# A hybrid decoder trunk: chunks of the input projection computed in turn, small with large

## The reference

```python
h = _rmsnorm(x, attn_norm[l])
proj = jnp.einsum('bsd,de->bse', h, w_in[l])     # one projection, columns split:
# differential attention (6 heads), gated linear attention (4 heads),
# latent attention (6 heads, low-rank queries 512 and keys/values 256 + rotary key 64)
x = x + jnp.einsum('bse,ed->bsd', mixed, w_out[l])
h2 = _rmsnorm(x, ffn_norm[l])
ff = jax.nn.silu(h2 @ w_gate[l]) * (h2 @ w_up[l])
x = x + ff @ w_down[l]
```

## Time and profile before

| | us |
|---|---|
| median of 3 runs | 2172.93 (2172.77 to 2174.07) |
| profiled execution | 2175.64 |
| its span | 2172.3 |
| granted TensorE clock, mean | 0.999 |
| busy: TensorE | 2159.1 (99%) |
| busy: VectorE | 1715.9 (79%) |
| busy: ScalarE | 1083.0 (50%) |

### The profile page before, as it was taken

One profiled execution on the slowest core, in us unless ns is written; L12 is line 12 of the kernel. 1 busy time (PEld: TensorE's weight loads), 2 busy tenths in 40 slices (PEclk: granted clock), 3 DMA queues, 4 the chain that ended last, 5 costly groups with the idle time before them and its releaser, 6 DMA issues.

```text
span 2172.3 us, 27182 instructions
## 1 busy us (share of the span) xinstructions
PE 2159.1 (99%) x10826; PEld 1843.7 (85%) x10826; DVE 1715.9 (79%) x1939; ACT 1083.0 (50%) x1145; POOL 22.2 (1%) x24
## 2 busy tenths in 40 slices
PE   9999999999999999999999999999999999999998
PEld 8899988888888888888888999888888888888886
DVE  5676774788899888889755866747888898888887
ACT  6454543554554455445443645445554454445544
POOL 0000000000000000000000000000000000000000
PEclk9999999999999999999999999999999999999999
DMA  7543455556556665665554434555565655665664
GB/s 265 179 137 117 148 173 194 178 198 205 194 195 197 201 198 196 204 198 194 194 189 158 151 113 158 173 178 192 194 197 198 203 193 194 198 207 194 198 206 158
DMA packets 221679, 402.77 MB, mean 185 GB/s; under 512 B 13440, under 2 KB 53664, under 8 KB 221472
## 3 DMA queue, kind: packets, MB, share of 16 engines
q1 hardware_dynamic: 220880, 400.90, 56.2%
q10 hardware_dynamic: 720, 0.78, 0.1%
HBM read 399.54 MB, written 2.10 MB: 185 GB/s over the span
## 4 chain that ended last, share of the span: by engine, by line
PE 95%; DVE 2%; DMA 1%; issue 1%; ACT 1%; SPq 0%; DVEq 0%; POOLq 0%; POOL 0%; ACTq 0%
PE bank L1021 19%; PE bank L1023 19%; PE bank L1022 19%; PE bank L698 10%; PE bank L700 10%; PE bank L699 10%; PE bank L658 3%; PE bank L823 1%; DMA stage<-in_w_down 1%; PE bank L764 0%; PE bank L887 0%; DMA stage<-in_w_in 0%; DVE w_lo L1551 0%; PE bank L875 0%; PE bank L765 0%
## 5 line engine op out<-in xcount | busy, mean ns | idle before, releaser
L1551 DVE TENSOR_TENSOR w_lo<-stage,w_hi 128x2048 fp32r<-128x2048 f32 (+4 forms) x318 | 678.0, 2134 | 266.7 <-ACT w_hi L1185 266.4
L1185 ACT ACTIVATE w_hi<-stage 128x2048 fp32r<-128x2048 f32 (+4 forms) x318 | 567.4, 1786 | 384.4 <-DMA stage<-in_w_down 191.3
L698 PE MATMUL bank<-w_hi,xt_hi 128*128 128x512 f32 (+4 forms) x1048 | 375.9, 359 | 2.0 <-DVE w_lo L1551 2.0
L700 PE MATMUL bank<-w_hi,xt_lo 128*128 128x512 f32 (+4 forms) x1048 | 368.9, 352 | 0.0
L699 PE MATMUL bank<-w_lo,xt_hi 128*128 128x512 f32 (+4 forms) x1048 | 368.7, 352 | 0.0
L1021 PE MATMUL bank<-w_hi,xt_hi 128*128 128x512 f32 x812 | 316.7, 390 | 0.5 <-DVE resid L2077 0.3
L1023 PE MATMUL bank<-w_hi,xt_lo 128*128 128x512 f32 x812 | 316.0, 389 | 0.0
L1022 PE MATMUL bank<-w_lo,xt_hi 128*128 128x512 f32 x812 | 315.9, 389 | 0.0
L1021 PE MATMUL bank<-w_hi,f_hi 128*128 128x512 f32 x696 | 271.3, 390 | 0.4 <-DVE f_lo L1966 0.4
L1023 PE MATMUL bank<-w_hi,f_lo 128*128 128x512 f32 x696 | 270.9, 389 | 0.0
L1022 PE MATMUL bank<-w_lo,f_hi 128*128 128x512 f32 x696 | 270.8, 389 | 0.0
(11 more groups left out here) (258 smaller groups left out, 2827.9 us busy)
## 6 DMA issues: line engine op xcount, KB each, us to landing
stage<-in_w_gate SPq DMA_DIRECT2D x176, 512.0 KB, 3.8
stage<-in_w_up SPq DMA_DIRECT2D x176, 512.0 KB, 4.7
stage<-in_w_down SPq DMA_DIRECT2D x174, 512.0 KB, 4.5
stage<-in_w_in SPq DMA_DIRECT2D x96, 384.0 KB, 3.7
stage<-in_w_out SPq DMA_DIRECT2D x64, 512.0 KB, 4.4
stage<-in_w_in SPq DMA_DIRECT2D x54, 512.0 KB, 4.5
stage<-in_w_in SPq DMA_DIRECT2D x16, 320.0 KB, 3.5
stage<-in_w_q_b SPq DMA_DIRECT2D x12, 384.0 KB, 3.8
```

What stands on the lines that cost most here:

```text
L698: pe.matmul(acc, a, wh[:, i, :], start=first and i == 0, stop=False)
L700: mm = pe.matmul(acc, b, wh[:, i, :], start=False, stop=last and i == len(kts) - 1)
L1185: act.activation(w_hi[s][:, 0:kts * cols], stage[s][:, 0:kts * cols], ACT.Copy).then_inc(hi_made[s], 1)
L1551: vec.tensor_tensor(w_lo[s][:, 0:kts * cols], stage[s][:, 0:kts * cols], w_hi[s][:, 0:kts * cols].bitcast(F32), ALU.subtract).then_inc(lo_ ...
```

## The change

The units of chunks 1 and 2 are done in turn, and those of chunks 3 and 4. Units 4 to 11 are now chunk 1, 2, 1, 2 and so on (320, 512, 320, 512 columns), units 12 to 19 chunk 3, 4, 3, 4 (512, 272). Chunk 1 ends with unit 10, chunk 2 with 11, chunk 3 with 18, chunk 4 with 19. The steps for the low-rank queries stand three places later; `angles` keeps its place at 13.

```diff
 EARLY_UNITS = [(c, range(k, k + width)) for c, (_, cols) in enumerate(EARLY) for width in [8 if cols <= 256 else 4]
                for k in range(0, KT, width)]
+EARLY_UNITS[4:12] = [unit for pair in zip(EARLY_UNITS[4:8], EARLY_UNITS[8:12]) for unit in pair]
+EARLY_UNITS[12:20] = [unit for pair in zip(EARLY_UNITS[12:16], EARLY_UNITS[16:20]) for unit in pair]
@@
-    put(7, ("qa_rms", 0))
-    put(8, ("qa_scale", 0))
+    put(10, ("qa_rms", 0))
+    put(11, ("qa_scale", 0))
     for b in range(3):
-        put(10 + b, ("qa_turn", b))
+        put(13 + b, ("qa_turn", b))
     put(13, ("angles", 0))
```

## The result

| | before | changed |
|---|---|---|
| median, us | 2173.87 (20 runs) | 2176.67 (19 runs) |
| ratio | | 1.0015, interval 1.0008 to 1.0021 |
| profiled execution: time, span | 2175.64, 2172.3 | 2178.01, 2176.2 |

A forecast was written before the change was run, and what follows sets the result against it. TensorE, busy for 99% of the span, was taken to bound the kernel. Old waits removed (-2.3 us) and new waits (+4.4 us) gave +2.1 us: from 2172.93 to 2175.0 us, 8-in-10 range 2170.6 to 2177.4.

The forecast's parts named there:

- Both waits at unit 20: TensorE's waits for w_lo where chunk 5 starts, 1.54 and 0.75 us in the two layers; both go, -2.3 us.
- The accumulators: Bank reuse between chunks: copy-outs done before the next chunk's first unit; cost nothing, at most 0.75 us a layer.
- A new wait ahead of unit 16: At place 13 the turn delays the angles and unit 16's rounding: about 2.2 us in each layer, +4.4 us.
- U: The moment when unit 13 leaves TensorE and the transposes start, from which the times up to unit 16 are counted.
- Sum: Whole kernel: -2.3 us for the old waits plus 4.4 us for the new ones, +2.1 us.
- Rival 3: TensorE's clock falls behind both new gaps, 2.9 us each: 2175.0 + 5.8 = 2180.8 us; chance 4%.
- Rival 1: At place 13 the angles hide after all, so only the old waits go: 2170.6 us; chance 10%.
- Rival 2: The wait at unit 20 stays beside the new one: 2177.3 us, or 2178.8 with chunk 3's copies; chance 10%.

The follow-up runs named there:

- the run with the first pair alone: Changed kernel with chunks 3 and 4 one after the other again: chunks 1 and 2 in turn, low-rank steps three places later; ratio to before 0.9996 (0.9987 to 1.0005).

## Why the prediction was right

- *Both waits at unit 20 go, -2.3 us*: right. Unit 20's load even took 5.2 us to ScalarE's start (94.71 to 99.93), not 5.96 as in the earlier trace rows, so that its low part was 1.8 us early, where 1.05 was reckoned.
- *The accumulators cost nothing, 0.3 us to spare at chunk 5*: right. VectorE's copy of chunk 3 ended at 104.83, 1.1 us ahead of unit 20. No wait came at units 5 to 11. It was closer than forecast there: unit 9's load took 6.9 us to ScalarE's start (41.93 to 48.80), more than the 6.33 that was taken for the slowest, and its low part, done at 53.0, was 1.2 us early, not 1.5.
- *A new wait ahead of unit 16, 2.2 us in both layers*: right in place, cause and size. From U = 77.12: turn's copy done at U + 2.45 (forecast 2.45), ScalarE's rounding at U + 7.54 (7.6), TensorE's start at U + 11.8 (12.0), wanted at U + 9.72 (9.75): 2.1 us. Putting the angles first removed it. The sine came 7.2 us after unit 13's end (some 7), and the groups waited 3.7 us in all for `w_lo` (about 4).
- *Sum +2.1 us*: right for the executions that list a clock of 0.999. Their median span is 2174.2 and 2174.0 in the two batches of the changed kernel and 2171.9 in the one before.
- *The time, 2175.0*: the median was 2176.67, inside the range (2170.6 to 2177.4) and 1.7 above the forecast. 0.9 of that is the starting point: three runs gave 2172.93 for the kernel before, twenty gave 2173.87.
- *Rival 3, the clock falls in the new gaps, 4%*: this was given too small a chance and too large a price, and taken as all or nothing. It comes in some 4 of 10 executions, in one of the two layers in both profiles, and costs 1.6 us, not 2.9: the price from the opening was for 5.8 us at the low clock, and it was 3.4. 13 of 30 times 1.6 is 0.7 us on average, as much as lies between the 2.8 us of the medians and the 2.1 forecast, though the interval of the ratio (1.7 to 4.6 us) is too wide to tell the two apart. The forecast put this at nothing; the range had room for it.
- *Rival 1, the angles hide*: didn't happen by itself; its time, 2170.6, is what the two kernels with the angles first come near to (2171.7 to 2172.2). *Rival 2*: nothing of it.

What stays open: why the fall comes in one execution and not in the next with the same wait, why the run with the first pair alone lists so many, and the 0.4 us that is scattered.

## What to carry to other kernels

A step that waits for another engine holds everything behind it in its queue, also work that was free to go. When steps are moved to a new place, read what else stands in that place and in which order: here a gain of 2.3 us was lost to one line of a list, and came back by swapping it. And a wait of TensorE can cost more than its length: with waits of 2.1 us, add the risk of a stretch at the low clock, here 0.7 us on average.

## What the runs showed of the hardware

- In both profiles of the changed kernel the granted clock fell to 1.2 GHz behind one of the two waits of 2.1 us, 1.5 or 0.5 us after TensorE had begun again, for 3.4 us. With waits of 5.7 us (one profile) it fell in both layers, while TensorE was idle.
- Executions that list a mean clock under 0.999: 17 of 41 with two waits of 2.1 us, 5 of 5 with 5.7 us, 1 of 33 without such waits, 6 of 86 with 1.5 and 0.75 us (the kernel before), but 4 of 11 with 0.8 us twice. The list does not say where the clock fell; in two of the other profiles it fell in the opening, at about 8 us.
- Eight matmuls whose result nobody reads, put in each wait of 2.1 us, brought this down to 1 of 22 and cost no time that I could see (median span 0.4 us under that of the changed kernel's executions with 0.999).
- A load of 1 MB for which ScalarE stood waiting took 5.0 us (unit 12 before, 52.36 to 57.38) to 6.9 us (unit 9 changed, 41.93 to 48.80) from its issue to ScalarE's start, in the first layer.
